# Coming blocks first on both sides of a weight change, and GpSimd makes the sums of coming weights, in a hybrid encoder step on one core

## The chip, the cores and the metric

The kernel runs on one core of a Trainium2 chip. The metric is the device time of one launch in microseconds. A core has a matrix engine (TensorE, in profiles PE; its weight loads are PEld), VectorE (DVE), ScalarE (ACT), GpSimd (POOL) and SyncE (SP, here a queue of DMA issues). Each engine runs its own list of instructions in order, and semaphores tie the lists together. SBUF is the on-chip memory, PSUM holds the eight banks into which TensorE adds its products.

## The reference

One layer of a streaming encoder for a prompt of 2048 tokens and a sample of 32 tokens, all in float32. The change touches only the combined input projection:

```
h = rmsnorm(x, p['norm1_w']) * (1 + sc1) + sh1
mq, mk, mv, mo, mi, mf, sq, sk, sv = split_proj(h @ p['w_in'])
...
q_b = rmsnorm(sq.reshape(B, T, SB_HEADS, SB_DIM), p['sb_q_norm_w'])
k_rows = rmsnorm(sk.reshape(B, T, SB_HEADS, SB_DIM), p['sb_k_norm_w'])
```

`h` has 1024 columns, `w_in` seven groups of 512 columns and eight gate columns. After it come the mLSTM heads, the stick-breaking attention, the output projection and the convolutional feed-forward part, which are the same before and after.

## The kernel before

Function `front` computes the projections. Group 0 of the weights is projected first, tile by tile (a tile is 128 tokens). The other six groups are taken in three pairs, (1,4), (5,3) and (6,2). Each pair is multiplied with the whole prompt in 8 units, so there are 24 units, w = 0 to 23. A unit takes two tiles of tokens and two groups of 512 columns as a 2 by 2 block product, and makes it of seven products instead of eight (Strassen's scheme in Winograd's form). The left factors are A11, A22, A12 and the sums S1 to S4 of quarters of `h`; the right ones, called cells here, are B11, B21, B22 and the sums T1 to T4 of quarters of the weights. The products are named P1 to P7 and stand on TensorE in the order P1, P5, P4, P6, P2, P7, P3.

Float32 is kept by parts: ScalarE copies a block to a rounded high part, VectorE subtracts it from the block for the low part, and a product is three passes (high by high, high by low, low by high) over four blocks of 128 rows, 12 matmuls. In each unit the left blocks of the next one are prepared: `left_sum_of` (VectorE), `left_high_of` (ScalarE), `left_low_of` (VectorE). The right blocks change only with the pair: `cell_high_of` and `cell_low_of` run in the unit before a change (w = 7 and 15, called leaving in the code: B11, T1, T4, T2) and in the first with new weights (w = 8 and 16, arriving: B21, T3, B22).

What ScalarE and VectorE do with the results: `seed_b` and `seed_c` copy a bank on which the next products build, `take_e`, `take_f` and `take_a` copy banks out, `add` makes the output tiles 1, 2 and 3 of a unit (tile 0 is the bank taken by `take_a`). From unit 8 on the tiles 0 and 2 are queries or keys of the attention. They are normalised by `norm_begin` (square and reduce) and `norm_end` (reciprocal and two products) on VectorE with `std` on ScalarE between. Then TensorE transposes them in the next unit (`turn`, four small matmuls, line 1354), ScalarE takes the high part (`take_turned`), VectorE the low part (`turned_low`, line 980), and GpSimd issues the two stores (`store_turned`). I write (w,0) and (w,1) for the two normalised tiles of unit w. A transpose waits for its tile, and also for the low part of the transpose before, since both use one bank:

```
pe.wait_ge(weighted, m + 1)
at_least(pe, turn_low, m)
```

The sums T1 to T4 of the next pairs' weights are made ahead, in eight events v = 0 to 7 in the units 0 to 5, 9 and 10. For each event SyncE loads four row blocks of weights (`load_event`, buffer `pw_rows`), TensorE multiplies the sample with them (`sample_product`, line 1366), VectorE overwrites them with the four sums (`event_sum`, line 899, 128x512 each), SyncE stores them (`store_event`, to `w_sums`), and the next load may be issued once the store has landed. Four more events, in units 11 to 14, have no sums. GpSimd fetches the sums and blocks back at a change (`renew`).

Nothing here is put in order by a scheduler: each engine's list is written out in the loops over w, and what stands in it is what the engine does next.

Of the kernel before, what the change touches and what calls it, by code (L numbers as in the profile page):

```python
# [124 lines left out]
def front(k, c, gc, dec, firstK, firstQ):  # L125
# [22 lines left out]
    LEFT_HIGHS = ("S1", "A11", "A22", "S2", "A12", "S3", "S4")  # L148
    LEFT_LOWS = ("A11", "A22", "S1", "A12", "S3", "S2", "S4")
# [78 lines left out]
    with ExitStack() as s:  # L228
# [77 lines left out]
        def product_of(w, name):  # L306

            return multiplied, 7 * w + PRODUCTS.index(name) + 1
# [62 lines left out]
        def _(sp):  # L371
# [57 lines left out]
            def store_out(w, j):  # L429
                if w >= FIRST and j in (0, 2):  # L430
                    sp.wait_ge(weighted, norm_tile(w, j // 2) + 1)
                elif j == 0:
                    sp.wait_ge(a_taken, w + 1)
                elif w < HALF and j in (1, 3):
                    sp.wait_ge(gated_out, 2 * w + j // 2 + 1)
                else:
                    sp.wait_ge(added, 3 * w + j)
# [69 lines left out]
            for w in range(UNITS):  # L507
# [18 lines left out]
                if w + 1 in EVENT_AT:  # L526
                    load_event(EVENT_AT[w + 1])
                store_out(w, 1)
# [3 lines left out]
                if w >= FIRST:  # L532
# [3 lines left out]
            store_out(UNITS - 1, 2)  # L536
# [9 lines left out]
        def _(act):  # L546
# [172 lines left out]
            for w in range(UNITS):  # L719
# [6 lines left out]
                if leaving:  # L726
                    cell_high_of(v, "B11")
                if arriving:
                    cell_high_of(w // HALF, "B21")
                if arriving and w > FIRST:  # L730
                    std(norm_tile(w - 1, 1))
                if more:
                    left_high_of("S1", n)
                take_e(w)
                if leaving:
                    cell_high_of(v, "T1")
                if arriving:
                    cell_high_of(w // HALF, "T3")
                if more:
                    left_high_of("A11", n)  # L740
                if w > FIRST:
                    take_turned(norm_tile(w - 1, 0))
                if more:
                    left_high_of("A22", n)
# [4 lines left out]
                if arriving:  # L749
                    cell_high_of(w // HALF, "B22")  # L750
                if more:
                    left_high_of("S2", n)
# [11 lines left out]
                if more:  # L764
                    left_high_of("A12", n)
                if w >= FIRST:
                    std(norm_tile(w, 0))
                if leaving:
                    cell_high_of(v, "T4")
                    cell_high_of(v, "T2")  # L770
                if more:
                    left_high_of("S3", n)
                if w < HALF:
                    gate_out(w, 1)
                if w >= FIRST and not leaving:
                    std(norm_tile(w, 1))
                if more:
                    left_high_of("S4", n)
# [8 lines left out]
        def _(dve):  # L787
# [100 lines left out]
            def event_sum(name, v_):  # L888
# [2997 lines left out]
```

## Time and profile before

| | us |
|---|---|
| median of 3 runs | 2980.31 (2975.06 to 2984.92) |
| the profiled execution | 2975.85 |
| its span | 2974.1 |
| TensorE busy | 2833.2, 95% of the span |
| VectorE busy | 2214.1, 74% |
| ScalarE busy | 1395.8, 47% |
| GpSimd busy | 556.2, 19% |

The time of an execution is the span plus what lies around it, here 1.75 us. The 24 units stand at 176.6 to 696 us of the span, and the attention begins at 709.4. A unit's first product P1 is the one written `pR<-pB,pA` after the product `pacc<-pB,pS` (P3) of the unit before. In the order of the units P5 is `pR<-pT,pS`, P4 `pR<-pT,pA`, P6 and P7 `pacc<-pT,pS`, and P2 again `pR<-pB,pA`. When products follow each other without a wait they start 2.72 us apart.

### The profile page before, as it was taken

To read this page: it belongs to the slowest core of one execution; us is meant where nothing else is said; L and a number is where in the kernel's file an instruction comes from. 1 tells how busy PE (TensorE), PEld (TensorE's weight loads), DVE (VectorE), ACT (ScalarE), POOL (GpSimd) and SP (SyncE) were. 2 spreads that over 40 slices of the span, in tenths; PEclk is the share of its full clock that TensorE was granted. 3 is DMA by queue.
4 is the path that set the end of the run, shared out by engine and by line. 5 is a ranking of instruction groups with operands and counts; after the bars stand their busy time and mean duration, and the time that the engine had idled before them with its cause. 6 is when DMAs were issued, how large, how long until landed. Compare 5 with 4: busy or idle time off the path is not lost.

```text
span 2974.1 us, 49846 instructions
## 1 busy us (share of the span) xinstructions
PE 2833.2 (95%) x16979; PEld 2446.7 (82%) x16979; DVE 2214.1 (74%) x3454; ACT 1395.8 (47%) x2729; POOL 556.2 (19%) x581
## 2 busy tenths in 40 slices
PE   6999999898999999999998999999999998999998
PEld 4777777686777888888887999999999997777776
DVE  3566687777998999796668777777877777887765
ACT  4644544435776888454555333333432224333332
POOL 3610011114666777220110000000000000000000
PEclk8999999998999999999999999999999999999999
DMA  7565666556422241696564444444667877655565
GB/s 267 200 222 201 211 234 203 184 177 159 128 59 59 60 99 43 216 338 195 187 215 161 150 150 150 152 153 153 209 219 230 262 235 254 195 189 188 179 209 186
DMA packets 359365, 541.47 MB, mean 182 GB/s; under 512 B 71058, under 2 KB 213976, under 8 KB 355478
## 3 DMA queue, kind: packets, MB, share of 16 engines
q1 hardware_dynamic: 337448, 467.81, 49.1%
q0 software_dynamic: 18112, 63.07, 6.2%
q10 hardware_dynamic: 3636, 8.45, 0.7%
q8 instruction: 93, 1.52, 0.2%
q14 instruction: 76, 0.62, 0.1%
HBM read 344.67 MB, written 194.55 MB: 181 GB/s over the span
## 4 chain that ended last, share of the span: by engine, by line
PE 45%; DVE 5%; DMA 5%; issue 1%; SPq 1%; ACT 1%; DVEq 0%; ACTq 0%
PE facc L3525 24%; PE facc L3655 6%; PE eacc L3504 6%; PE dacc L3655 4%; DMA y_out<-dres 1%; DMA fsums<-sums_d 1%; PE mpT L3678 1%; PE mpm L3687 1%; DVE fV L3036 1%; DMA w_out_plain<-w_out 1%; PE mpS L3697 1%; PE eyT L3487 1%; PE exT L3517 0%; DVE fV L3032 0%; DMA dsample_act<-act_d 0%
## 5 line engine op out<-in xcount | busy, mean ns | idle before, releaser
L3525 PE MATMUL facc<-fright,fsums 128*128 128x416 f32 x2112 | 419.3, 354 | 17.3 <-ACT facc L2591 7.2
L3525 PEld LDWEIGHTS facc<-fright,fsums 128*128 128x128 f32 x2112 | 398.7, 190 | 24.5 <-issue 16.3
L1720 DVE TENSOR_TENSOR_SCAN aC<-aB,aC,a 128x512 f32<-128x512 f32 (+3 forms) x326 | 362.8, 1113 | 12.5 <-ACT aB L1676 0.9
L1780 POOL TENSOR_TENSOR aS<-aS,aC 128x512 f32<-128x512 f32 (+3 forms) x326 | 335.0, 1035 | 154.0 <-DVE aC L1720 147.4
L3525 PE MATMUL facc<-fright,fwH 128*128 128x416 f32 x1056 | 290.1, 356 | 11.8 <-DVE fU L3020 9.9
L3525 PEld LDWEIGHTS facc<-fright,fwH 128*128 128x128 f32 x1056 | 199.3, 190 | 17.5 <-issue 12.2
L2980 DVE TENSOR_TENSOR fwL<-fraw,fwH 128x1024 fp32r<-128x1024 f32 x86 | 93.4, 1086 | 148.9 <-ACT fwH L2591 148.8
L2591 ACT ACTIVATE fU<-facc 128x416 f32<-128x416 f32 x132 | 67.4, 513 | 287.2 <-PE facc L3525 287.2
L1800 PE MATMUL a_z<-ak,aq 128*128 128x512 f32 (+2 forms) x616 | 199.7, 406 | 0.9 <-DMA ak<-qk_T 0.9
L1676 ACT ACTIVATE aB<-a_z 128x512 f32<-128x512 f32 (+3 forms) x326 | 180.3, 553 | 32.2 <-PE a_z L1800 18.9
L1826 PE MATMUL a_x<-ident,aS 128*128 128x128 f32 x1106 | 182.4, 281 | 10.5 <-ACT aA L1685 8.2
L3525 PE MATMUL facc<-fh,fwH 128*128 128x416 f32 x704 | 189.8, 351 | 0.0
L3525 PE MATMUL facc<-fright,fwL 128*128 128x416 f32 x528 | 186.4, 353 | 0.0
L1681 ACT ACTIVATE aS<-a_z 128x512 f32<-128x512 f32 (+3 forms) x326 | 182.2, 559 | 0.0
L1826 PEld LDWEIGHTS a_x<-ident,aS 128*128 128x128 f32 x1106 | 123.7, 141 | 53.9 <-issue 32.3
L1845 PEld LDWEIGHTS a_out<-aA,av 128*64 128x64 f32 x2176 | 123.4, 137 | 40.8 <-issue 31.0
L1845 PE MATMUL a_out<-aA,av 128*64 128x128 f32 x2176 | 155.2, 281 | 0.0
L1395 PE MATMUL pacc<-pT,pS 128*128 128x512 f32 x576 | 144.8, 401 | 5.6 <-DVE pT L911 2.9
L2591 ACT ACTIVATE dS<-dS_plain 128x512 fp32r<-128x512 f32 (+1 forms) x96 | 57.3, 597 | 187.1 <-DVE dS_plain L3109 61.9
L1395 PE MATMUL pR<-pB,pA 128*128 128x512 f32 x576 | 138.6, 389 | 1.3 <-issue 1.1
L547 ACT ACTIVATE pS<-pS_plain 128x512 fp32r<-128x512 f32 x96 | 60.7, 632 | 164.6 <-DVE pS_plain L928 63.2
L1395 PEld LDWEIGHTS pacc<-pT,pS 128*128 128x128 f32 x576 | 107.2, 191 | 35.5 <-issue 9.7
(438 smaller groups left out, 6351.3 us busy)
## 6 DMA issues: line engine op xcount, KB each, us to landing
sums_d<-fsums SPq DMA_DIRECT2D x88, 512.0 KB, 3.0
fsums<-sums_d SPq DMA_DIRECT2D x88, 512.0 KB, 4.6
fraw<-w_up SPq DMA_DIRECT2D x66, 512.0 KB, 4.1
proj_out<-pout SPq DMA_DIRECT2D x96, 256.0 KB, 4.3
ppart<-h_d SPq DMA_DIRECT2D x46, 512.0 KB, 4.6
dres<-x_d SPq DMA_DIRECT2D x92, 256.0 KB, 3.4
mwa<-w_ada SPq DMA_DIRECT2D x16, 1024.0 KB, 6.8
dpart<-act_d SPq DMA_DIRECT2D x32, 512.0 KB, 3.8
```

The source lines that it names most:

```text
L1395: op = mm_(banks[name], lefts[one][:, a, i], cell(other, b)[:, i], start=(name in ("P1", "P5", "P4") and i == 0 and m == 0), stop=(i == NK ...
L1676: nc.scalar.activation(part(B, RB, n), part(Z, NZ, n), ACT.Sigmoid, scale=-1.0).then_inc(pass_ready, 1)
L1681: nc.scalar.activation(part(S, RS, n), part(Z, NZ, n), ACT.Sigmoid).then_inc(stop_ready, 1)
L1720: v.tensor_tensor_scan(buf[:, a:b][:, ::-1], part(B, RB, n)[:, ::-1], nought[:, 0:width(n)], buf[:, b:b + 1], ALU.mult, ALU.add).then_inc( ...
L1780: nc.gpsimd.tensor_tensor(at, at, buf[:, a + 1:b + 1], ALU.mult).then_inc(w_ready, 1)
L1800: mm = nc.tensor.matmul(to, q[:, i * P:(i + 1) * P], keys[:, span], start=(half == 0), stop=(half == 1), skip_group_check=True)
L1826: mm = nc.tensor.transpose(X[:, n % NX, j * P:(j + 1) * P], src[:, j * P:(j + 1) * P], c["ident"][:])
L1845: mm = nc.tensor.matmul(O[e * SD:(e + 1) * SD, u % 2, at:at + P], V[:, h % 2, b], weight[:, j * P:(j + 1) * P], start=lead, stop=(g == 0 a ...
L2591: copy = lambda to, at: nc.scalar.activation(to, at, ACT.Copy)
L3504: mm = nc.tensor.matmul(acc[:, 1 - i.u, cols], a[:, i.u, kk], w[:, kk, cols], start=(kk == 0 and n == 0), stop=(kk == KD - 1 and n == len( ...
L3525: mm = nc.tensor.matmul(bank, a[:, kk], b[:, kk], start=(begins and kk == 0 and m == 0), stop=(kk == count - 1 and m == 2), skip_group_che ...
L3655: mm = nc.tensor.matmul(banks[name], a[:, i], b, start=(name in ("P1", "P5", "P4") and i == 0 and m == 0), stop=(i == len(WINDOW[w]) - 1 a ...
```

## The change

It has four parts.

1. In the two units of a weight change ScalarE and VectorE have another order. The coming cells and left blocks stand earlier (T1 on ScalarE after `take_f`, T3 right after B21, A12 and its like before T4, T2 after S3), and the high parts of units 8, 9, 16 and 17 are made in the order S1, A11, A22, A12, S2, S3, S4.
2. The tile (15,1) is normalised later in unit 16 and transposed after P1 of unit 17, not after P2 of unit 16. Its `take_turned` and `turned_low` stand at the head of unit 17. GpSimd fetches T4 for the last pair before it stores tile (14,0), and B21 before (14,1).
3. The last unit makes its products in the order P1, P4, P6, P2, P7, P5, P3, normalises tile 2 and adds it before the others, and stores as they come.
4. `event_sum` moves from VectorE to GpSimd. There the sums of events 0 to 3 stand after the stores of blank rows, those of 4 and 5 after `store_rows`, those of 6 and 7 after the stores of tiles (8,0) and (9,0).

```
+    CHANGE_HIGHS = ("S1", "A11", "A22", "A12", "S2", "S3", "S4")
+    LAST_PRODUCTS = ("P1", "P4", "P6", "P2", "P7", "P5", "P3")
...
@@ ScalarE, loop over the units @@
+                if w > FIRST and (w - 1) % HALF == 0 and w - 1 > FIRST:
+                    take_turned(norm_tile(w - 2, 1))
+                if leaving or arriving:
+                    if leaving:
+                        cell_high_of(v, "B11")
+                    else:
+                        cell_high_of(w // HALF, "B21")
+                        cell_high_of(w // HALF, "T3")
                     left_high_of("S1", n)
+                    take_e(w)
+                    if w > FIRST:
+                        take_turned(norm_tile(w - 1, 0))
+                    take_f(w)
+                    if leaving:
+                        cell_high_of(v, "T1")
+                    seed_c(w)
+                    if n in TAKEN_AT:
+                        take_sample(TAKEN_AT[n])
+                    if arriving:
+                        cell_high_of(w // HALF, "B22")
+                    left_high_of("A11", n)
+                    left_high_of("A22", n)
+                    if arriving and w > FIRST:
+                        std(norm_tile(w - 1, 1))
+                    take_a(w)
+                    if leaving and w > FIRST:
+                        take_turned(norm_tile(w - 1, 1))
+                    left_high_of("A12", n)
+                    left_high_of("S2", n)
+                    if leaving:
+                        cell_high_of(v, "T4")
+                    if w >= FIRST:
+                        std(norm_tile(w, 0))
+                    left_high_of("S3", n)
+                    if w < HALF:
+                        gate_out(w, 1)
+                    if leaving:
+                        cell_high_of(v, "T2")
+                    else:
+                        std(norm_tile(w, 1))
+                    left_high_of("S4", n)
+                    if w < HALF:
+                        gate_out(w, 3)
+                    continue
...
@@ VectorE, loop over the units @@
+                if w > FIRST and (w - 1) % HALF == 0 and w - 1 > FIRST:
+                    turned_low(norm_tile(w - 2, 1))
                 if leaving:
+                    left_sum_of(1, n)
+                    if w > FIRST:
+                        turned_low(norm_tile(w - 1, 0))
                     cell_low_of(n // HALF, "B11")
+                    cell_low_of(n // HALF, "T1")
+                    left_low_of("A11", n)
+                    left_low_of("A22", n)
+                    left_sum_of(2, n)
+                    left_low_of("S1", n)
+                    left_low_of("A12", n)
+                    if w >= FIRST:
+                        norm_begin(w, 0)
+                    if w > FIRST:
+                        turned_low(norm_tile(w - 1, 1))
+                    add(w, 1)
+                    add(w, 2)
+                    cell_low_of(n // HALF, "T4")
+                    left_sum_of(3, n)
+                    if w >= FIRST:
+                        norm_end(w, 0)
+                    cell_low_of(n // HALF, "T2")
+                    left_low_of("S3", n)
+                    add(w, 3)
+                    left_sum_of(4, n)
+                    left_low_of("S2", n)
+                    left_low_of("S4", n)
+                    continue
                 if arriving:
                     cell_low_of(w // HALF, "B21")
-                if arriving and w > FIRST:
-                    norm_begin(w - 1, 1)
-                if more:
                     left_sum_of(1, n)
...
                     cell_low_of(w // HALF, "T3")
+                    if w > FIRST:
+                        turned_low(norm_tile(w - 1, 0))
+                        norm_begin(w - 1, 1)
+                    cell_low_of(w // HALF, "B22")
                     left_low_of("A11", n)
+                    left_low_of("A22", n)
+                    left_sum_of(2, n)
+                    left_low_of("S1", n)
+                    left_low_of("A12", n)
+                    if w > FIRST:
+                        norm_end(w - 1, 1)
+                    norm_begin(w, 0)
+                    add(w, 1)
+                    add(w, 2)
+                    left_sum_of(3, n)
+                    left_low_of("S3", n)
+                    norm_end(w, 0)
+                    norm_begin(w, 1)
+                    add(w, 3)
+                    left_sum_of(4, n)
+                    left_low_of("S2", n)
+                    left_low_of("S4", n)
+                    continue
...
@@ GpSimd @@
+            for n in range(4):
+                event_sums(n)
             store_rows()
+            for n in range(4, NK + 2):
+                event_sums(n)
             for name in CELLS[len(AHEAD):]:
                 renew(1, name)
             for m in range(NORMS):
-                store_turned(m)
                 if m == norm_tile(2 * HALF - 2, 0):
                     renew(2, "T4")
+                store_turned(m)
+                if m in (0, 2):
+                    event_sums(NK + 2 + m // 2)
...
@@ TensorE, unit @@
-                for name in PRODUCTS:
+                for name in products(w):
...
+                    if name == "P1" and w % HALF == 1 and w - 1 > FIRST:
+                        turn(norm_tile(w - 2, 1))
-                    if name == "P5" and w > FIRST:
+                    if name == ("P5" if w < UNITS - 1 else "P4") and w > FIRST:
                         turn(norm_tile(w - 1, 0))
+                    if name == "P5" and w == UNITS - 1:
+                        turn(norm_tile(w, 0))
...
-                    if name == "P2" and w > FIRST:
+                    if name == "P2" and w > FIRST and w % HALF:
                         turn(norm_tile(w - 1, 1))
```

Three places in the lists show it. VectorE in unit 16, before, where the low part of the transposed tile (15,1) stands behind `norm_begin(16,0)`. The names are the left blocks (pA, pS), the squares (`pacc<-pout`), the low part (`pturn_low<-pacc`) and the output tiles (pout).

```order
L944 TENSOR_TENSOR pA<-ppart,pA 128x512
L961 TENSOR_TENSOR pacc<-pout 128x512
L963 TENSOR_REDUCE pnst<-pacc 128x8
L980 TENSOR_TENSOR pturn_low<-pacc,pturn 128x512
L954 TENSOR_TENSOR pout<-pE,pacc 128x512
L949 TENSOR_TENSOR pout<-pout,pacc 128x512
L933 TENSOR_TENSOR pS_plain<-ppart 128x512
L944 TENSOR_TENSOR pS<-pS_plain,pS 128x512
```

And now, at the end of unit 16 and the head of unit 17:

```order
L986 TENSOR_TENSOR pout<-pE,pacc 128x512
L967 TENSOR_TENSOR pS_plain<-ppart,pS_plain 128x512
L975 TENSOR_TENSOR pS<-pS_plain,pS 128x512 x2
L1001 RECIPROCAL pnst<-pnst 128x8
L1003 TENSOR_TENSOR pout<-pout,pnst 128x512
L1007 TENSOR_TENSOR pout<-pout,pnw 128x512
L1012 TENSOR_TENSOR pturn_low<-pacc,pturn 128x512
L959 TENSOR_TENSOR pS_plain<-ppart 128x512
L975 TENSOR_TENSOR pA<-ppart,pA 128x512
```

The low part has moved behind the whole of unit 16 and behind `norm_end(16,1)`, and stands right ahead of the first left sum of unit 17.

TensorE from the last product of unit 16 into unit 17, before:

```order
L1395 MATMUL pacc<-pB,pS 128x512 x12
L1395 MATMUL pR<-pB,pA 128x512 x12
L1395 MATMUL pR<-pT,pS 128x512 x12
L1354 MATMUL pacc<-ident,pout 128x128 x4
L1395 MATMUL pR<-pT,pA 128x512 x12
```

And now:

```order
L1483 MATMUL pacc<-pB,pS 128x512 x12
L1483 MATMUL pR<-pB,pA 128x512 x12
L1442 MATMUL pacc<-ident,pout 128x128 x4
L1483 MATMUL pR<-pT,pS 128x512 x12
L1442 MATMUL pacc<-ident,pout 128x128 x4
L1483 MATMUL pR<-pT,pA 128x512 x12
```

A second transpose stands in unit 17 ahead of P5, that of (15,1); the one after P5, of (16,0), waits for its low part.

GpSimd from the stores of blank rows on, before:

```order
L1188 DMA proj_out<-pblank 96x512 x6
L1193 DMA ug_d<-pturn 68x128 x4
L1195 DMA m_out<-pm_end 8x1x1
L1212 DMA pT_plain<-w_sums 128x4x512 x2
L1212 DMA pB_plain<-w_in 128x4x512
```

And now (`pw_rows` are the rows of weights that become their sums):

```order
L1268 DMA proj_out<-pblank 96x512 x6
L1245 TENSOR_TENSOR pw_rows<-pw_rows 128x512 x16
L1273 DMA ug_d<-pturn 68x128 x4
L1275 DMA m_out<-pm_end 8x1x1
L1245 TENSOR_TENSOR pw_rows<-pw_rows 128x512 x8
L1292 DMA pT_plain<-w_sums 128x4x512 x2
L1292 DMA pB_plain<-w_in 128x4x512
L1292 DMA pT_plain<-w_sums 128x4x512
L1292 DMA pB_plain<-w_in 128x4x512
L1283 DMA qk_T<-pturn 128x4x128
L1284 DMA qk_T<-pturn 128x4x128
L1245 TENSOR_TENSOR pw_rows<-pw_rows 128x512 x4
```

Sixteen sums come in, then eight, then twice four behind the two DMAs of a transposed tile.

## Rows read from the trace of the kernel before

**Rows 1.** Busy time by stretches: stretch, length, busy us (instructions), granted clock, DMA.

```profile
core 0: us, PE busy (x) PEld busy (x) DVE busy (x) ACT busy (x) POOL busy (x), PEclk, DMA share, GB/s
340.50:366.20 25.70, 20.15 (x85) 15.46 (x84) 20.37 (x21) 16.39 (x20) 0.75 (x1) 1.00 0.47 159
...
494.30:521.50 27.20, 22.75 (x93) 18.45 (x92) 20.09 (x29) 11.82 (x19) 5.66 (x8) 0.87 0.54 176
521.50:552.60 31.10, 23.01 (x93) 18.13 (x92) 25.28 (x29) 17.53 (x22) 3.08 (x5) 0.89 0.61 219
552.60:573.20 20.60, 20.47 (x94) 16.51 (x93) 14.24 (x25) 10.64 (x18) 2.99 (x4) 1.00 0.50 160
...
595.30:675.90 80.60, 80.58 (x369) 66.18 (x368) 62.69 (x105) 32.39 (x64) 11.95 (x16) 1.00 0.55 170
```

**Rows 2.** TensorE's timeline in unit 8: start, duration, instruction, [idle before, releaser].

```profile
359.35 3.00 PE L1395 MATMUL pacc<-pT,pS 128*128 128x512 f32 x12 [2.94 <-DVE pT L911]
```

**Rows 3.** TensorE's timeline in units 15 and 16.

```profile
513.00 1.09 PE L1354 MATMUL pacc<-ident,pout 128*128 128x128 f32 x4 [4.45 <-DVE pturn L980]
513.74 5.18 PE L1395 MATMUL pacc<-pT,pS 128*128 128x512 f32 x12
...
533.96 1.11 PE L1354 MATMUL pacc<-ident,pout 128*128 128x128 f32 x4 [6.84 <-DVE pout L975]
534.73 4.95 PE L1395 MATMUL pR<-pT,pA 128*128 128x512 f32 x12
```

**Rows 4.** Timelines of VectorE, SyncE's queue and TensorE, units 0 and 1.

```profile
193.85 2.74 DVE L899 TENSOR_TENSOR pw_rows<-pw_rows 128x512 f32<-128x512 f32 x4
...
196.62 0.33 SPq L427 DMA_DIRECT2D w_sums<-pw_rows  x1
...
200.56 1.76 SPq L421 DMA_DIRECT2D pw_rows<-w_in  x4
...
207.48 1.07 PE L1366 MATMUL pR<-pw_rows,h_plain 128*32 128x256 f32 x16
```

**Rows 5.** GpSimd's timeline, the first projection and unit 9.

```profile
105.86 1.29 POOL L1167 TENSOR_TENSOR pT_plain<-pturn,pT_plain 128x512 f32<-128x512 f32 x1
107.22 1.30 POOL L1169 TENSOR_TENSOR pT_plain<-pturn,pT_plain 128x512 f32<-128x512 f32 x1
...
380.85 0.75 POOL L1204 DMA_DIRECT2D qk_T<-pturn  x1
```

**Rows 6.** Timelines of GpSimd and VectorE, first projection.

```profile
143.50 4.68 POOL L1157 TENSOR_TENSOR h1L<-h_plain,h1H 128x1024 fp32r<-128x1024 f32 x1
149.75 2.37 POOL L1157 TENSOR_TENSOR h1L<-h_plain,h1H 128x1024 fp32r<-128x1024 f32 x1 [1.57 <-DMA h_d<-h_plain]
...
143.63 2.34 DVE L885 TENSOR_TENSOR pT<-pT_plain,pT 128x1024 fp32r<-128x1024 f32 x2
```

**Rows 7.** Timelines of SyncE's queue and TensorE, units 9 and 10.

```profile
367.99 1.85 SPq L421 DMA_DIRECT2D pw_rows<-w_in  x4
...
374.94 1.07 PE L1366 MATMUL pR<-pw_rows,h_plain 128*32 128x256 f32 x16
...
389.19 1.96 SPq L421 DMA_DIRECT2D pw_rows<-w_in  x4
...
396.53 1.07 PE L1366 MATMUL pR<-pw_rows,h_plain 128*32 128x256 f32 x16 [0.24 <-DMA pw_rows<-w_in]
```

**Rows 8.** VectorE's timeline, units 15 to 17.

```profile
502.51 0.69 DVE L975 TENSOR_TENSOR pout<-pout,pnw 128x512 f32<-128x512 f32 x1
...
547.41 2.28 DVE L911 TENSOR_TENSOR pB<-pB_plain,pB 128x2048 fp32r<-128x2048 f32 x1
549.61 0.68 DVE L944 TENSOR_TENSOR pS<-pS_plain,pS 128x512 fp32r<-128x512 f32 x1
550.21 0.68 DVE L944 TENSOR_TENSOR pA<-ppart,pA 128x512 fp32r<-128x512 f32 x1
...
562.49 0.69 DVE L975 TENSOR_TENSOR pout<-pout,pnw 128x512 f32<-128x512 f32 x1
```

**Rows 9.** Timelines of ScalarE and VectorE, last unit.

```profile
683.88 0.58 ACT L547 ACTIVATE pacc<-pR 128x512 f32<-128x512 f32 x1
...
701.87 0.69 DVE L980 TENSOR_TENSOR pturn_low<-pacc,pturn 128x512 fp32r<-128x512 f32 x1 [1.90 <-ACT pturn L547]
```

More of the change, by code:

```diff
@@ L436, in store_out @@
                 else:
-                    sp.wait_ge(added, 3 * w + j)
+                    sp.wait_ge(added, 3 * w + (2 if j == 1 and w == UNITS - 1 else j))
                 sp.dma_start(d["proj_out"][group_of(w, j), tok(tile_of(w, j)), :], out(w, j)).then_inc(out_stored[j][w % 2], 16)
@@ L741, in _ @@
+                if not more:
+                    take_turned(norm_tile(w - 1, 0))
+                    take_f(w)
+                    seed_c(w)
+                    take_a(w)
+                    take_turned(norm_tile(w - 1, 1))
+                    std(norm_tile(w, 0))
+                    std(norm_tile(w, 1))
+                    take_e(w)
+                    break
+                left_high_of("S1", n)
+                take_e(w)
+                left_high_of("A11", n)
                 if w > FIRST:
@@ L742, in _ @@
                     take_turned(norm_tile(w - 1, 0))
-                if more:
-                    left_high_of("A22", n)
+                left_high_of("A22", n)
                 take_f(w)
@@ L748, in _ @@
                     take_sample(TAKEN_AT[n])
[L749 to L752, printed above, removed]
+                left_high_of("S2", n)
                 if w == 4:
@@ new lines, in _ @@
+                    norm_end(w, 0)
[5 more added lines that the diff above has]
+                    continue
+                if not more:
+                    turned_low(norm_tile(w - 1, 0))
+                    norm_begin(w, 0)
+                    norm_end(w, 0)
+                    turned_low(norm_tile(w - 1, 1))
+                    add(w, 2)
+                    norm_begin(w, 1)
+                    norm_end(w, 1)
+                    add(w, 1)
+                    turned_low(norm_tile(w, 0))
+                    add(w, 3)
+                    turned_low(norm_tile(w, 1))
+                    break
@@ L1078, in _ @@
+                left_sum_of(1, n)
+                left_low_of("A11", n)
                 if w > FIRST:
                     turned_low(norm_tile(w - 1, 0))
-                if arriving and w > FIRST:
-                    norm_end(w - 1, 1)
-                if more:
-                    left_low_of("A22", n)
+                left_low_of("A22", n)
                 if TAKEN_AT.get(w, NN) < NN:
                     sample_squares(TAKEN_AT[w])
-                if more:
-                    left_sum_of(2, n)
@@ L1137, in _ @@
                     gate_columns()
-            norm_end(UNITS - 1, 1)
-            for m in range(NORMS - 2, NORMS):
-                turned_low(m)
         @block.gpsimd
@@ L1425, in _ @@
                 unit(w)
-            for m in range(NORMS - 2, NORMS):
-                turn(m)
+            turn(NORMS - 1)
     k.keep(first_head_in)
```

118 lines of the change are left out of this document (44 added, 74 removed).

## The prediction, as it was made before the result was known

> **What bounds the kernel now.** All the edits lie in the first projections, 176.6 to 709.4 us, so I read the busy time by stretches first. The reader should see TensorE within half a microsecond of full in the long steady stretches, and idle time in four places: 25.70 us for 20.15 us of work around unit 8, 27.20 for 22.75 in unit 15, 31.10 for 23.01 in unit 16 [rows 1], and a tail after the last unit. A steady unit without weight rows takes 20.1 us (80.60 us for four, same rows); in the two bad units the granted clock falls to 0.87 and 0.89. So TensorE bounds the stage, and only what ends a TensorE wait counts. Next, TensorE in order of time. At the first change of weights the longest wait is 2.94 us, for VectorE's low half of T3 [rows 2]. At the second, a transpose waits 4.45 us for another transpose's low half and one waits 6.84 us for a normalised tile; the product after the first took 5.18 us where 3.0 is usual [rows 3]. The losses are 6.7 us (25.7 less 19.0) in unit 8, 7.0 in unit 15 and 10.9 in unit 16. Last I read what feeds these, VectorE and the queues.
>
> **The change, part by part.** Times below are absolute positions in the trace of before, and D is how much later TensorE stands.
>
> *The sums of coming weights.* VectorE made four in 2.74 us beginning right at the end of the row product [rows 4]. GpSimd needs 1.30 each for the same size, 5.2 us [rows 5]. In units 1 to 5 VectorE reached its sums some microseconds late, so GpSimd, which starts when the product ends, is as early. Not in unit 0: there VectorE began at 193.85, so GpSimd ends near 199.2 instead of 196.59. The chain behind it has no slack: sums, store issued at 196.62, next load at 200.56 (3.9 later), product at 207.48 [rows 4]. In SyncE's queue nothing else holds that load by then. D after unit 1 is +2.6. From below: the rows may have landed up to 0.6 before they were used, and GpSimd may be as quick as VectorE, which gives 0; from above 3.2, if the first of the four takes half a microsecond more.
>
> In units 9 and 10 GpSimd must first store a transposed tile, because its list has store_turned(0) and (2) ahead of the sums. It issued the second of its two DMAs at 380.85 [rows 5], so the four sums run from 381.6 to 386.8 at best. VectorE works beside them. The row of a GpSimd difference that took 4.68 us, against 2.37 alone, while VectorE made two differences of 1.17, shows the two in turn and not at once [rows 6]. VectorE has one or two such instructions to make here (an A12 low half, the squares), so I take +1.6: 388.4. The store lands 3.9 later, 392.3, against a load issued at 389.19. TensorE used these rows at 396.53 after a wait for them [rows 7]: D +3.0 here. The ends are 1.4, without the collision, and 3.8, with twice of it. The same chain in unit 10 comes out only 0.2 to 1 us later than before, which a TensorE already 3 us late does not feel. What VectorE saves (2.74 us eight times) buys nothing, since TensorE did not wait for VectorE in those units.
>
> The Trainium skill (SBUF — State Buffer, section Who interferes with whom) says that a VectorE instruction with two SBUF inputs and a GpSimd instruction that reads SBUF exclude each other for the whole instruction. The trace agrees, 4.68 being 2.37 plus 2.34 us; without contention this term would be 1.6 us smaller, +1.4 in place of +3.0.
>
> *First change, units 7 to 9.* ScalarE now takes T4 some 1.6 us earlier, but T2 only after S3 and a gate, and S4, the second gate and seed_b(8) stand behind T2. P6 and P2 of unit 8 so start about 1.4 us later than before. T3's high half then follows B21's at once on ScalarE, and its low half stands ahead of A11 on VectorE; P7 starts at 357.6 instead of 359.35 [rows 2], P3 and unit 9 also 1.8 us earlier. Then its first transpose waits 1 us for a tile that VectorE normalises at the old time. Then the rows of weights: those of unit 9 were requested at 367.99 and used at 374.94 [rows 7], and that request stands behind the third left sum, which moves by +0.3. I take 0, with ends -1.8 and +0.6.
>
> *Second change, units 15 to 17.* First what goes: the left sum and the turned low half come ahead of B11 and T1 on VectorE, so the 4.45 us wait goes and with it the slow P7 (5.18 for 3.0). TensorE ends unit 15 at 514.2 instead of 521.5. From here VectorE sets the pace. Its instructions step at 0.60 (512 wide) and 2.20 (2048 wide: 547.41 to the next at 549.61), a norm_begin takes 1.34, a norm_end 1.57 [rows 8]. Its list from the end of norm_end(14,1), 502.51 + 0.6 = 503.1: sum 0.6; a wait until 505.5, while ScalarE does S1 (0.78 after the sum's start), E and the turned tile at 0.5 each; turned low 0.6; B11, T1 4.5; five short and a pause 3.2; norm_begin 1.3; turned low and two adds 1.8; T4 2.2 (519.1); sum, norm_end 2.2 (521.3); T2 when ScalarE has done S3 and T2, 522.3, to 524.5; S3, add, sum 2.0; then S4 and seed_b on ScalarE end at 527.5. P6 of unit 16 starts at 527.65, 3.0 late. ScalarE's B21 takes 1.84, and the low half 2.2: 531.6, P2. sum, T3 low: 534.4. ScalarE reaches B22 behind T3, S1, E, the turned tile, F, the seed and the sample at 535.2, and ends at 537.1; B22's low half ends at 539.35, against 547.41 + 2.28 = 549.69 before [rows 8]. TensorE is 10.3 us ahead there, with waits of 1.7, 3.0, 1.2, 0.5 and 1.7 us behind it.
>
> Now what is late next. In unit 17 the second transpose, of tile (16,0), may write its bank only when the low half of (15,1) has been taken. That low half now stands behind VectorE's whole rest of unit 16. Before, from A12's low half at 550.21 to the last instruction of norm_end(16,1), 562.49, plus 0.61, are 12.9 us [rows 8]. The new list adds norm_end(15,1), 1.57; the low half only changes its place; and A11, A22, a sum and S1 ahead of A12 add 2.6. That is 17.05: 539.35 becomes 556.4. TensorE gets to that transpose at 539.45 + 8.65 (P3, P1, a transpose, P5; 2.72 a product) = 548.1, and stands 8.4 us. And what follows runs at half clock, as after the 6.84 us wait: a transpose of 1.1 us and a P4 of 4.95 [rows 3]. The transpose starts at 556.5, P4 at 557.3, P6 at 562.1, P2 at 564.8, a transpose, P7 and P3 end at 573.4, where unit 18 starts; before it started at 573.2 [rows 1]. So all of the 10.3 us is given back. Term +0.2. The ends: -4 if the clock holds and VectorE's list is 1.5 us shorter, +3 if the waits of unit 16 also slow a product or the fetch of T4 or B22 is late. Nothing hides this wait: behind the transpose TensorE has P4, and P4 needs only what is long ready.
>
> *The last unit.* P6 comes third instead of fourth. It needs seed_b, which ended on ScalarE at 684.46 [rows 9], and so starts at 684.60 as before, while P5, which used to fill 678.6 to 681.3, now comes after P7. TensorE ends 2.7 us later. Against it, tile 2 is added and normalised without waiting for P3; the last transpose waits for the low half of (23,0), 700.4, and the last low half starts at 702.2 against 701.87 [rows 9]. +0.4, with ends -2 and +2.7.
>
> **Sum.** 2.6 + 3.0 + 0 + 0.2 + 0.4 = +6.2 us. The profiled execution took 2975.85 us, 1.75 of it outside the span; the sum on it is 2982.1. The median of before is 2980.31, 4.5 above that execution, so a median of the new kernel should be 2986.5, +0.2%. About 0.3% (9 us) is what a measurement can tell here from no change.
>
> **Rivals.**
> *The second change keeps its gain.* The low half of (15,1) would be taken in time, or TensorE would meet it within a couple of microseconds. Then the 10.3 us stay, the 2 us that unit 18 takes over a steady unit (22.1 against 20.1) go, and if GpSimd's sums land in time too the 5.6 us as well: 2975.85 + 6.2 - 12.3 - 5.6, about 2964 on the profiled execution, 2968 as a median. For it: the two long waits of rows 3 do disappear. Against it: the count of VectorE's list above, which needs no guess at a new duration. 0.2.
>
> *The clock falls in units 16 and 17 (slower).* Five waits of 0.5 to 3 us stand within 20 us, then 8.4 us. In the trace the granted clock was 0.89 of 31 us where the single wait was 6.84 [rows 1, 3], and full around unit 8 with 2.94. If four more products go at 5.2 instead of 3.0 us that is +9, and +3 from late rows and the end: 2975.85 + 6.2 + 12, as a median 2998. It decides once two of the products P6, P2, P7 and P3 of unit 16 take over 4 us. 0.2.
>
> *The moved sums cost nothing.* The rows land as before, because GpSimd starts the moment the product ends and the copies have slack that I don't see. Then +0.6: 2981. For it: units 1 to 5. Against it: the three visible waits for these rows of 0.2 to 0.7 us. 0.15.
>
> My forecast has 0.45. Split by the 9 us bound, with the run-to-run spread of the three runs (10 us): the first rival is faster in nearly all of its 0.2, the second slower in all of its 0.2, and the forecast's own range, 2978 to 2994, puts 0.04 beyond the slower side. Faster 0.19, within 0.3% 0.56, slower 0.25. The range that leaves out one tenth on either side reaches to the rivals' values, 2968 to 2998.
>
> **What would show it.** TensorE's row product of unit 1 at about 210 and waiting for its rows; that of unit 10 near 402; the product after unit 15's transpose at full clock; a transpose in unit 17 that waits some 8 us for a turned low half on VectorE, its product P4 slow; P6 of the last unit waiting 2.9 us for ScalarE. I am wrong if unit 17's transpose waits under 3 us, or if rows of weights cause no wait.

## The result and the profile after

| | before | changed |
|---|---|---|
| median of 12 runs each, us | 2980.07 | 2983.90 |
| the profiled execution, its span, us | 2975.85, 2974.1 | 2986.12, 2984.4 |
| ratio of the times, 95% interval | | 1.002 (1.001 to 1.0029) |

The changed kernel is 0.2% slower, within the 0.3% that I called no change. One of its twelve executions took 4592 us at a granted clock of 0.56; it is left out of the ratio, and without it the median is 2983.50. Of the 10.3 us between the two profiled spans 7.6 lie in the stretch that the change touches (from TensorE's first P1 of unit 0 to the attention's first matmul, 532.86 us before and 540.48 after). 2.6 lie ahead of any edit: unit 0 starts at 179.19 instead of 176.59, and over the executions of this study that start moved between 175.6 and 181.1. I therefore compare lengths from here on, not positions.

The page's first part, of the changed kernel. GpSimd has gained 46.6 us of busy time, and VectorE has lost only 3.5 of its 2214.1, though it gave up eight times 2.74 us [rows 4]:

```profile
## 1 busy us (share of the span) xinstructions
PE 2833.7 (95%) x16979; PEld 2446.8 (82%) x16979; DVE 2210.6 (74%) x3422; ACT 1396.8 (47%) x2729; POOL 602.8 (20%) x613
```

Busy time by stretches of the changed kernel, cut at its own units: 0 and 1, 8, 9 to 11, then 15, 16, 17, 18, and 23 up to the attention. Columns as in [rows 1]:

```profile
179.19:226.86 47.67, 42.97 (x201) 33.01 (x201) 26.89 (x42) 20.71 (x35) 16.07 (x17) 0.96 0.64 225
...
347.19:371.70 24.51, 19.95 (x86) 15.46 (x84) 17.22 (x17) 15.21 (x19) 0.75 (x1) 1.00 0.48 172
371.70:442.47 70.77, 64.58 (x325) 50.42 (x324) 61.27 (x88) 26.19 (x52) 19.63 (x19) 1.00 0.61 203
506.27:526.27 20.00, 20.00 (x93) 16.55 (x92) 17.12 (x25) 12.63 (x19) 4.24 (x6) 1.00 0.83 267
526.27:554.44 28.17, 22.27 (x89) 16.77 (x88) 24.54 (x28) 15.74 (x21) 4.51 (x6) 0.94 0.61 212
554.44:584.77 30.33, 22.17 (x97) 18.11 (x96) 20.40 (x35) 12.32 (x21) 3.55 (x5) 0.89 0.36 117
584.77:604.77 20.00, 20.00 (x93) 16.55 (x92) 15.61 (x27) 8.09 (x16) 2.89 (x5) 1.00 0.49 159
...
684.77:719.67 34.90, 23.12 (x102) 18.38 (x100) 19.16 (x33) 6.93 (x15) 7.51 (x12) 0.89 0.42 136
```

The same lengths, unit by unit (distance from P1 to the next unit's P1), of both kernels and of the experiments, tell where each microsecond is. Units 12 to 14 take 63.8 to 64.1 in all.

| length, us | 0, 1 | 2 to 7 | 8 | 9 to 11 | 15 | 16 | 17 | 18 | 19 to 22 | 23 and tail | all |
|---|---|---|---|---|---|---|---|---|---|---|---|
| before | 42.94 | 120.98 | 25.69 | 64.29 | 27.23 | 31.09 | 20.56 | 22.08 | 80.66 | 33.54 | 532.86 |
| changed | 47.67 | 120.33 | 24.51 | 70.77 | 20.00 | 28.17 | 30.33 | 20.00 | 80.00 | 34.90 | 540.48 |
| changed again | 46.71 | 119.88 | 24.51 | 70.68 | 20.00 | 28.17 | 30.66 | 20.00 | 80.00 | 33.33 | 538.05 |
| e1 | 42.94 | 120.63 | 24.48 | 66.07 | 20.00 | 28.15 | 31.24 | 20.00 | 80.00 | 33.73 | 531.04 |
| e2 | 46.79 | 120.86 | 25.99 | 68.42 | 27.40 | 31.08 | 20.54 | 22.13 | 80.37 | 33.13 | 540.51 |
| e3 | 45.86 | 120.02 | 24.49 | 70.83 | 20.00 | 28.20 | 23.54 | 22.10 | 80.38 | 34.78 | 534.00 |
| e4 | 48.81 | 120.07 | 24.50 | 70.90 | 20.00 | 28.15 | 30.95 | 20.00 | 80.00 | 32.72 | 539.90 |
| e5 | 43.86 | 120.89 | 24.48 | 66.18 | 20.00 | 28.21 | 23.52 | 22.10 | 80.37 | 33.37 | 526.78 |
| e6 | 42.90 | 120.64 | 22.28 | 65.88 | 20.00 | 26.45 | 24.25 | 21.40 | 80.38 | 33.59 | 521.85 |
| e7 | 42.95 | 119.98 | 24.52 | 66.03 | 20.00 | 28.14 | 30.20 | 20.00 | 80.00 | 34.97 | 530.59 |

Read changed against before: +4.7 in units 0 and 1, -1.2 in unit 8, +6.5 in 9 to 11, then -7.2 and -2.9 in 15 and 16, +9.8 in 17, -2.1 and -0.7 behind it, +1.4 at the end.

TensorE's waits in the whole stage of the changed kernel, first part of that view (what was waited for: us in total, times, longest):

```profile
PE pacc L1483 <- ACT pacc L559: 9.3, 4, 3.0
PE pacc L1442 <- DVE pturn_low L1012: 8.2, 1, 8.2
PE pR L1454 <- DMA pw_rows<-w_in: 7.0, 5, 3.1
PE pacc L1442 <- DVE pout L1007: 4.2, 4, 1.5
```

The rows of weights were waited for 1.2 us in all before and now 7.0; one transpose waits 8.2. The places of both in TensorE's timeline:

```profile
213.23 1.69 PE L1454 MATMUL pR<-pw_rows,h_plain 128*32 128x256 f32 x16 [3.09 <-DMA pw_rows<-w_in]
...
382.67 1.07 PE L1454 MATMUL pR<-pw_rows,h_plain 128*32 128x256 f32 x16 [1.11 <-DMA pw_rows<-w_in]
...
406.51 1.07 PE L1454 MATMUL pR<-pw_rows,h_plain 128*32 128x256 f32 x16 [1.29 <-DMA pw_rows<-w_in]
...
429.94 1.07 PE L1454 MATMUL pR<-pw_rows,h_plain 128*32 128x256 f32 x16 [1.10 <-DMA pw_rows<-w_in]
...
533.41 0.66 PE L1442 MATMUL pacc<-ident,pout 128*128 128x128 f32 x4 [1.54 <-DVE pout L1007]
...
539.80 4.24 PE L1483 MATMUL pacc<-pT,pS 128*128 128x512 f32 x12 [2.98 <-ACT pacc L559]
543.91 3.31 PE L1483 MATMUL pR<-pB,pA 128*128 128x512 f32 x12
...
551.60 3.00 PE L1483 MATMUL pacc<-pB,pS 128*128 128x512 f32 x12 [1.38 <-issue]
...
568.70 1.09 PE L1442 MATMUL pacc<-ident,pout 128*128 128x128 f32 x4 [8.16 <-DVE pturn_low L1012]
569.44 4.14 PE L1483 MATMUL pR<-pT,pA 128*128 128x512 f32 x12
...
693.31 4.18 PE L1483 MATMUL pacc<-pT,pS 128*128 128x512 f32 x12 [2.50 <-ACT pacc L559]
```

The first four are the row products of units 1, 9, 10 and 11. The waits of [rows 3] are gone, and in unit 16 (526.27 to 554.44) stand 1.54, 2.98 and 1.38 us instead. The transpose at 568.70 is that of (16,0); the 8.16 us ahead of it are the largest wait of the stage. P6 at 693.31 is that of the last unit, waiting for ScalarE's seed.

### The profile page after: what moved, and what is told of

The parts are those of the page before. It is cut to its first block, busy times and chain, and to the rows that moved or that the text cites. A ratio compares the mean times of both kernels' runs of the same rounds, so it can differ in the third digit from the quotient of the medians.

```text
span 2984.4 us, 49870 instructions
## 1 busy us (share of the span) xinstructions
PE 2833.7 (95%) x16979; PEld 2446.8 (82%) x16979; DVE 2210.6 (74%) x3422; ACT 1396.8 (47%) x2729; POOL 602.8 (20%) x613
## 4 chain that ended last, share of the span: by engine, by line
PE 46%; DVE 5%; DMA 5%; issue 1%; SPq 1%; ACT 1%; DVEq 0%; ACTq 0%
PE facc L3616 24%; PE facc L3746 6%; PE eacc L3595 6%; PE dacc L3746 4%; DMA y_out<-dres 1%; DMA fsums<-sums_d 1%; PE mpT L3769 1%; DMA dres<-x_d 1%; DVE fV L3127 1%; DMA w_out_plain<-w_out 1%; PE mpm L3778 1%; PE mpS L3788 1%; PE eyT L3578 1%; DVE fV L3123 0%; DVE fV L3132 0%
## 5 line engine op out<-in xcount | busy, mean ns | idle before, releaser
L1917 PE MATMUL a_x<-ident,aS 128*128 128x128 f32 x1106 | 182.1, 281 | 10.1 <-ACT aA L1776 8.2
```

What stands on the lines that cost most here:

```text
L1917: mm = nc.tensor.transpose(X[:, n % NX, j * P:(j + 1) * P], src[:, j * P:(j + 1) * P], c["ident"][:])
```

## The experiments

The changed kernel was built up and taken apart in pieces. The lengths are in the table above. Ratios are to the kernel before.

**The changed kernel once more**, for the spread of its lengths.

> The changed kernel as it is, run beside the next three on one chip, since e3 and e4 came out 4 to 6 us faster in time than the length of their units says. If that is a matter of the chip, this run is near +0.1% here with a stage of 540.5 us; if it belongs to e3 and e4, it is at +0.2% again.

2981.37 us, ratio 1.001 (1.000 to 1.002), stage 538.05. Of the stage's lengths units 8 and 15 to 22 repeat within 0.4 us, units 0 and 1 and the tail differ by 1.0 and 1.6. The two stages differ by 2.4 us, so a single execution tells the stage no better than that, and single units between 15 and 22 much better. The run was also to show whether the times of e3 and e4, below, are better than their stages for a reason of the chip. It came out at the +0.1% named for that case, but its interval also holds the +0.2% of the other, so it does not decide.

**e1: the sums back on VectorE**, all else as changed.

```
@@ VectorE, in the other units @@
+    event = EVENT_AT.get(w, SUMMED)
+    if event < SUMMED:
+        for name in ("T1", "T3", "T2", "T4"):
+            event_sum(name, event)
@@ GpSimd @@
-    for n in range(4):
-        event_sums(n)
     store_rows()
-    for n in range(4, NK + 2):
-        event_sums(n)
...
-    if m in (0, 2):
-        event_sums(NK + 2 + m // 2)
```

> The changed kernel with the event sums back on VectorE, in its place of before (behind S1's low half); all else as changed. Theory (the moved sums cost about 9 us: 4.4 in unit 1, 4 to 5 around units 9 to 11): no wait for rows over 0.8 us, no VectorE instruction of 3.6 us, the 24 units and what follows to the attention take 540.5 - 9 = 531.5 us, and the time is about 1.5 us under before. Rival (the new order at the changes costs it, the sums nothing): the stage stays near 540 and the time near +0.2%.

2973.21 us, ratio 0.9978 (0.9966 to 0.9989), stage 531.04. Against the changed kernel units 0 and 1 give back 4.7 us and units 9 to 11 another 4.7: the whole loss by GpSimd's sums, 9.4 us, where the prediction had 5.6. The stage fits the expected 531.5, the time is further under before than expected (6.6 us for 1.5). Of the waits for rows 0.96 us in unit 9 stays, more than the 0.8 that I had allowed, so that one comes with the new order of the first change. The 8.21 us wait in unit 17 stays, and so do the gains of 15 and 16.

**e2: the kernel before, with the sums on GpSimd**, the same edit in the other direction.

```
@@ VectorE @@
-    if event < SUMMED:
-        for name in ("T1", "T3", "T2", "T4"):
-            event_sum(name, event)
@@ GpSimd @@
+    for n in range(4):
+        event_sums(n)
     store_rows()
+    for n in range(4, NK + 2):
+        event_sums(n)
...
+    if m in (0, 2):
+        event_sums(NK + 2 + m // 2)
```

> The kernel before with one edit: the event sums on GpSimd, placed as in the changed kernel. Theory: unit 1 waits some 3 us for its rows, units 10 and 11 about 1 to 2 us each for rows and for the normalised tile; the stage takes 532.9 + 9 = 542 us, the time is +0.3% on before. Rival (the sums are hidden without the new order): stage 533 to 535, time as before.

2985.32 us, ratio 1.0023 (1.0012 to 1.0033), stage 540.51, 7.7 above before: +3.9 in units 0 and 1, +4.1 in 9 to 11, together 8.0. TensorE's row product of unit 1 in this kernel:

```profile
214.48 1.94 PE L1373 MATMUL pR<-pw_rows,h_plain 128*32 128x256 f32 x16 [2.47 <-DMA pw_rows<-w_in]
216.35 3.54 PE L1402 MATMUL pacc<-pT,pS 128*128 128x512 f32 x12
```

It waits for the rows, and is itself slow (1.94 for 1.07 us), as is the product behind it. So the late rows of units 1, 10 and 11 come with the fourth part of the change alone (units 10 and 11 wait 1.18 and 1.09 us for them here).

**e3: the low part of (15,1) earlier**, behind the third left sum of unit 16, with ScalarE's copy of it. Nothing else differs from the changed kernel.

```
@@ ScalarE, unit 17 and unit 16 @@
-    if w > FIRST and (w - 1) % HALF == 0 and w - 1 > FIRST:
-        take_turned(norm_tile(w - 2, 1))
...
     take_a(w)
+    if arriving and w > FIRST:
+        take_turned(norm_tile(w - 1, 1))
@@ VectorE, unit 17 and unit 16 @@
-    if w > FIRST and (w - 1) % HALF == 0 and w - 1 > FIRST:
-        turned_low(norm_tile(w - 2, 1))
...
     left_sum_of(3, n)
+    if w > FIRST:
+        turned_low(norm_tile(w - 1, 1))
```

> The changed kernel, but the low half of the transposed tile (15,1) (with ScalarE's copy) stands inside unit 16's list, behind the third left sum, not at the head of unit 17. Theory: the 8.2 us wait of the transpose (16,0) falls to about 2.3, until norm_end(16,0) is done; its P4 runs at full clock; stage 540.5 - 6.8 = 533.7, the time equals before to 0.05%. Rival (VectorE is simply behind here, whatever the order): the wait stays above 6 us or comes back as a wait of P6, stage 539 or more.

2975.73 us, ratio 0.9989 (0.9979 to 0.9999), stage 534.00. TensorE's timeline in unit 17:

```profile
559.17 0.66 PE L1442 MATMUL pacc<-ident,pout 128*128 128x128 f32 x4 [1.94 <-DVE pout L1007]
559.58 3.01 PE L1483 MATMUL pR<-pT,pA 128*128 128x512 f32 x12
...
581.27 0.66 PE L1442 MATMUL pacc<-ident,pout 128*128 128x128 f32 x4 [1.01 <-DVE pout L1007]
```

Busy time of units 16 and 17 of e3, columns as above, at full clock in both:

```profile
523.00:551.13 28.13, 20.75 (x89) 15.69 (x88) 24.50 (x28) 15.70 (x21) 4.52 (x6) 1.00 0.62 217
551.13:574.67 23.54, 21.18 (x98) 16.77 (x97) 17.67 (x31) 11.42 (x20) 2.99 (x4) 1.00 0.45 151
```

One subtraction of 0.69 us moved up on VectorE, and ScalarE's copy with it, takes the wait from 8.16 to 1.94 us and P4 from 4.14 to 3.01. Unit 17 is 6.8 us shorter. Unit 18 is 2.1 longer again, with the wait of 1.01 us that stood there before and that the changed kernel did not have: while TensorE stands for 8 us VectorE catches up with it, and where it does not stand, VectorE is late again one unit on. I had not allowed for that: with 2.5 us back in units 18 to 22 the early low part is worth 4.3 us and not 6.8, and the stage fits the expected 533.7 because units 0 and 1 happened to take 1.8 us less here, which the edit does not touch.

**e4: the last unit in its old order**, the rest as changed.

```
-    return PRODUCTS if w < UNITS - 1 else LAST_PRODUCTS
+    return PRODUCTS
@@ VectorE, last unit @@
-    norm_end(w, 0)
...
+    norm_end(w, 0)
+    add(w, 1)
...
+    add(w, 3)
```

> The changed kernel with the last unit's products in the order of before (P1, P5, P4, P6, P2, P7, P3), its lists following. Theory: the 2.5 us wait of P6 and the slow product behind it go, a wait of 3.5 us for the last transposes comes back; stage 540.5 - 1.4 = 539.1, not to be told from the changed kernel by time. Rival (the new last order gains in the tail what it loses at P6): stage 541 or more.

2981.95 us, ratio 1.0005 (0.9994 to 1.0016), stage 539.90. From the last P1 to the attention it takes 32.72 us. Over all the runs of the table that length is 33.54, 33.13, 32.72, 33.37 and 33.59 with the old order (mean 33.3) and 34.90, 33.33, 33.73, 34.78 and 34.97 with the new one (mean 34.3). So the new order costs about 1.1 us in the mean, less than its own spread. The waits alone do not say why, since they come to nearly the same: the old order waits 3.44 to 3.47 us for the last transpose, the new one 1.02 or 1.03 there and 2.50 to 2.69 for the seed ahead of P6. What differs is the speed of P6 behind that wait. It took 2.98 and 2.96 us in the changed kernel once more and in e1, with 33.33 and 33.73 us to the attention, as in the old order. It took 4.18, 4.29 and 4.49 in the changed kernel, e3 and e7, with 34.90, 34.78 and 34.97. The stage of e4 is only 0.6 us under the changed kernel's, between the expected 539.1 and the rival's 541, because units 0 and 1 took 48.81 us in this execution.

**e5: e1, e3 and e4 in one kernel**: of the change there remains the new order of both weight changes, with the low part early.

> The changed kernel with three parts taken back or put right: sums on VectorE, the low half of (15,1) in unit 16, the last unit in its old order. Theory (the three terms add): stage 531.0 - 6.5 - 0.6 = 524 us, 9 us under before, time -0.3% or better. Rival (VectorE has the sums to make again and catches TensorE at another place): stage 528 or more.

2969.73 us, ratio 0.9972 (0.9959 to 0.9985), stage 526.78 for an expected 524, between that and the rival's 528. 0.9 of the difference is a wait for rows in unit 0, which no other run with VectorE's sums had; another 1.8 was in the expectation, which took e3's gain with its short units 0 and 1. The pieces add up: from the changed kernel's 540.5, 8.4 go in the sums' units, 6.8 in unit 17, 1.5 at the end, 2.5 come back in units 18 to 22, and 0.6 in 2 to 7.

**e6: e5 with B21 ahead of S4.** The wait of 2.98 us ahead of P6 in unit 16, and of 2.30 in unit 8, is for `seed_b`, which stood behind S4 on ScalarE. Here it and B21's high part come ahead of S4.

```
@@ ScalarE @@
-    seed_b(w)
+    if not arriving:
+        seed_b(w)
...
-    cell_high_of(w // HALF, "B21")
...
+    seed_b(n)
+    cell_high_of(v, "B21")
     left_high_of("S4", n)
```

> e5 with ScalarE's seed_b and the high half of B21 for the first unit with new weights ahead of S4 in the unit before. Theory: at the second change B21's low half no longer waits for ScalarE (1.6 us idle of VectorE in the changed kernel) and P6 waits 0.5 us less; stage 1.5 to 2 us under e5, 522. Rival (the fetched B21 lands late, or VectorE's count alone sets the pace): stage as e5 or longer.

2966.27 us, ratio 0.9962 (0.9948 to 0.9976), stage 521.85. This kernel is faster than both: by 0.4% than before, and by 0.5% than the changed one as measured on the same chip (0.9962 to 1.001). TensorE around P6 of units 8 and 16:

```profile
353.84 3.02 PE L1494 MATMUL pacc<-pT,pS 128*128 128x512 f32 x12 [1.28 <-DVE pS L988]
...
529.51 3.02 PE L1494 MATMUL pacc<-pT,pS 128*128 128x512 f32 x12 [2.46 <-DVE pS L988]
532.41 2.98 PE L1494 MATMUL pR<-pB,pA 128*128 128x512 f32 x12
...
550.98 0.66 PE L1453 MATMUL pacc<-ident,pout 128*128 128x128 f32 x4 [1.98 <-DVE pout L1020]
551.39 4.58 PE L1494 MATMUL pR<-pT,pA 128*128 128x512 f32 x12
```

The waits ahead of P6 now name VectorE's low part of a left sum, since S4's high part comes later, and they are shorter by 1.0 and 0.5 us. The other 1.2 us in each come behind P6: P2 starts 2.90 us after it, where in the changed kernel it starts 4.11 after (543.91 less 539.80), held by B21, whose low part ends on VectorE at 543.80. 0.7 of it went again in unit 17, where the product after the transpose took 4.58 us.

**e7: only the sums of events 1 to 5 on GpSimd**, those of 0, 6 and 7 on VectorE.

```
@@ VectorE @@
-    if event < SUMMED:
+    if event < SUMMED and event not in [1, 2, 3, 4, 5]:
@@ GpSimd @@
+    event_sums(1)
+    event_sums(2)
+    event_sums(3)
     store_rows()
+    event_sums(4)
+    event_sums(5)
```

> e1 with the sums of events 1 to 5 on GpSimd, those of 0, 6 and 7 on VectorE. Theory: these five are hidden on either engine, stage as e1, 531.0 within 0.5, no wait for rows in units 2 to 4. Rival (each moved sum costs TensorE something): 3 to 5 us more than e1.

2973.48 us, ratio 0.9986 (0.9976 to 0.9997), stage 530.59, as e1, and no wait for rows stands in units 2 to 4. These five are hidden on either engine; the loss is made by the three events (0, 6 and 7) whose chain has no slack.

## Why the prediction was right, and where it was not

The time came out as forecast (2983.9 for 2986.5, by the sum +6.2 us in the stage for a measured +7.6 and, once more, +5.2). That the number is so near is in part luck. The sums on GpSimd cost 8.0 to 9.4 us where I had 5.6, and the last unit 1.0 more than forecast in this execution; a gain of 2.7 us behind unit 17, which the forecast did not have, made up for about half of that.

*Sums in units 0 and 1, +2.6.* The chain went as described and GpSimd began on time, 17.26 us after unit 0's P1 as VectorE had. But it took longer:

```profile
196.45 6.07 POOL L1245 TENSOR_TENSOR pw_rows<-pw_rows 128x512 f32<-128x512 f32 x4 [2.88 <-PE pR L1454]
...
389.12 5.95 POOL L1245 TENSOR_TENSOR pw_rows<-pw_rows 128x512 f32<-128x512 f32 x4
```

6.07 us, not the 5.2 of four times 1.30 [rows 5]. SyncE's queue stored them at once and requested the next rows 4.2 us later:

```profile
202.54 0.33 SPq L437 DMA_DIRECT2D w_sums<-pw_rows  x1
...
206.69 1.76 SPq L431 DMA_DIRECT2D pw_rows<-w_in  x4
```

The row product came 3.15 us later than before, at the upper end that I gave (3.2). On top the clock fell: granted 0.96 over units 0 and 1, and the product that waited took 1.69 us for 1.07, the P6 behind it 4.01. Together +4.7. The five executions with all sums on GpSimd have +2.9 (e3), +3.8 (changed again), +3.9 (e2), +4.7 and +5.9 (e4), and the two lowest are those in which no product behind the wait was slow. The term was mis-sized by 0.3 to 3.3 us, and a fall of the clock stood only in the rival about units 16 and 17.

*Units 9 and 10, +3.0, and unit 11, nothing.* This is the step that failed. e1 isolates it: without GpSimd's sums units 9 to 11 take 66.07 us, with them 70.77, +4.7. Unit 9 hardly differs (23.36 and 23.52). Unit 10 has +2.5 for my +3.0, and unit 11 has +2.0 for nothing. I had written that the chain in unit 10 comes "only 0.2 to 1 us later than before, which a TensorE already 3 us late does not feel". It came later still, and unit 11 waits 1.10 us for its rows and 0.84 for a tile. GpSimd's sums in unit 10 took 5.94 us, as in unit 9, and VectorE lost time as well, where I had let it save 2.74 us an event. VectorE of the changed kernel in unit 9, beside the sums of 389.12 to 395.07:

```profile
388.62 3.60 DVE L975 TENSOR_TENSOR pS<-pS_plain,pS 128x512 fp32r<-128x512 f32 x1
392.14 1.77 DVE L975 TENSOR_TENSOR pA<-ppart,pA 128x512 fp32r<-128x512 f32 x1
393.83 1.78 DVE L993 TENSOR_TENSOR pacc<-pout 128x512 f32<-128x512 f32 x1
395.65 0.69 DVE L995 TENSOR_REDUCE pnst<-pacc 128x8 f32<-128x512 f32 x1
```

The same instructions in e1, with VectorE's own sums among them:

```profile
382.82 0.69 DVE L988 TENSOR_TENSOR pS<-pS_plain,pS 128x512 fp32r<-128x512 f32 x1
383.43 2.74 DVE L943 TENSOR_TENSOR pw_rows<-pw_rows 128x512 f32<-128x512 f32 x4
386.09 0.68 DVE L988 TENSOR_TENSOR pA<-ppart,pA 128x512 fp32r<-128x512 f32 x1
386.69 0.69 DVE L1006 TENSOR_TENSOR pacc<-pout 128x512 f32<-128x512 f32 x1
387.42 0.69 DVE L1008 TENSOR_REDUCE pnst<-pacc 128x8 f32<-128x512 f32 x1
```

From the start of the first to the start of the reduction it is 7.03 us with the sums on GpSimd and 4.60 with them on VectorE. VectorE is slower for having given the work away. The three instructions lost 5.1 us together and the sums would have cost 2.7. That comes back as the transposes' waits in units 10 and 11 (0.98 and 0.84 us, both for a normalised tile of VectorE; e2 has 0.94 and 0.93, e1 and e7 none there), and with the rows' waits of 1.29 and 1.10 it makes 4.2 of the +4.5.

The Trainium skill (SBUF — State Buffer, section Who interferes with whom) says that a VectorE instruction with two inputs in SBUF contends with a GpSimd instruction that reads SBUF, and that one with at most one SBUF input, outside the 2-port modes, does not. The rows agree in unit 9: the three with two SBUF inputs took 3.60, 1.77 and 1.78 us. The reduction started after GpSimd's end and tells nothing. VectorE beside the group of unit 0 (196.45 to 202.52) has both kinds:

```profile
197.51 0.78 DVE L975 TENSOR_TENSOR pA<-ppart,pA 128x512 fp32r<-128x512 f32 x1 [0.97 <-ACT pA L559]
199.29 0.69 DVE L986 TENSOR_TENSOR pout<-pE,pacc 128x512 f32<-128x512 f32 x1 [1.00 <-PE pacc L1483]
199.90 0.68 DVE L981 TENSOR_TENSOR pout<-pout,pacc 128x512 f32<-128x512 f32 x1
```

The two adds with an input in PSUM (`pacc`) took their usual time, as the skill has it. But the difference with two SBUF inputs took only 0.78 us here for 1.77 in unit 9, so what such an instruction loses is not fixed, and no run shows what sets it. I had used that rule for GpSimd's end and not for VectorE's.

*First change, 0.* Right within its ends. P6 of unit 8 starts 1.8 us later than before (forecast 1.4) and P7 1.3 earlier (1.8), so unit 8 is 1.2 us shorter; in e1, which has no delay by the sums, unit 9 takes 2.1 back, with waits of 0.89 us for a tile and 0.96 for rows. Units 8 to 11 of e1 are 0.6 us longer than before's, the upper end that I gave. No run undid this part alone, so that split rests on e1's and before's lengths.

*Second change, +0.2.* Right in size and in place. Unit 15 at 20.0 us (-7.2, forecast -7.3), P6 of unit 16 waits 2.98 (3.0), units 15 and 16 together -10.1 (-10.3), the transpose in unit 17 waits 8.16 (8.4) and P4 takes 4.14 (4.95), so units 15 to 17 together are -0.4. The count of VectorE's list held. The transpose of (16,0) started 42.43 us after unit 16's P1, and by the prediction's positions 42.3 (556.5 less 514.2). Why that is so late shows on VectorE in the changed kernel:

```profile
549.21 2.29 DVE L942 TENSOR_TENSOR pB<-pB_plain,pB 128x2048 fp32r<-128x2048 f32 x1 [0.67 <-ACT pB L559]
551.42 1.29 DVE L975 TENSOR_TENSOR pA<-ppart,pA 128x512 fp32r<-128x512 f32 x2
...
567.26 0.69 DVE L1007 TENSOR_TENSOR pout<-pout,pnw 128x512 f32<-128x512 f32 x1
567.87 0.68 DVE L1012 TENSOR_TENSOR pturn_low<-pacc,pturn 128x512 fp32r<-128x512 f32 x1
```

From the end of B22's low half at 551.4 VectorE works without an idle time of a microsecond until the low part, which starts at 567.87 and is done 17.1 us after that end; I had 17.05. e3, which moves nothing but this low part and its copy, shows that it is their place in the lists.

*Units 18 to 22, nothing.* -2.7 measured. The wait of 8 us lets VectorE catch up, so the small waits of units 18 and 19 go; e3 and e5, without the long wait, have them again. The prediction put this gain with the rival in which unit 17 does not wait, which is the wrong way round.

*The last unit, +0.4.* The named wait came, 2.50 us for 2.9, and the length is between the ends that I gave: +1.4 in this execution, about +1.1 as a mean over ten. In the two executions with P6 at its usual speed it is -0.2 and +0.2 of before's; the rest is the slow P6, which the term did not have.

*The rivals.* The second change did not keep its gain. The clock fell in one product of unit 16 (P6, 4.24 us), not in two, so that rival stayed short of its own condition. That one product cost nothing either: unit 16 took 28.17 us with it and 28.20 in e3, where its granted clock was full, since P2 waits for B21 in any case. Even in e4, with P6 at 5.46 us, the unit took 28.15. The moved sums cost 8.0 (e2 against before) to 9.4 us (against e1), not nothing.

What stays open: e1, e3 and e4 are by their times 4 to 6 us better than their stages say (e1: -6.6 us by the ratio, -1.8 by the stage), while e2 and e6 agree within 1 us, and in e5, e7 and the changed kernel once more the time is about 2 us better than the stage. The rest of the program, from the attention on, is the same code, but took 2258 to 2265 us in the single profiled executions of the study. So one execution cannot place those 5 us, and their cause stays open.

## What to carry to other kernels

Before work is moved from one elementwise engine to the other, look at what the giver does meanwhile and at how many inputs its instructions read from SBUF: in unit 9 VectorE gave 2.7 us of work away and lost 5.1 beside it. Ask of each moved block not its busy time but the chain behind it: all eight have a store and a load behind them, and for five of them that chain has slack, so that they could go to either engine at no cost that shows; for three it has none, and these cost 8 to 9 us. And when a wait on a shared buffer is moved into a later unit, count the list of the engine that frees it down to the instruction that frees it; one subtraction made 8.5 us earlier was worth 6.8 us in its unit, and 4.3 when the next five units are counted.

## What the runs showed of the hardware that I had not expected

A VectorE difference of 128x512 took 3.60 us instead of 0.69 when it met GpSimd's sums, 2.8 times the 1.30 us of one GpSimd operation, though it had started 0.5 us before them. GpSimd's four took 5.6 to 6.4 us over the eight events, for 5.2.

The half clock (1.2 GHz) does not follow from the length of a single wait. P6 of unit 16 took 4.24 us after 2.98 in the changed kernel, and P7 of unit 8 took 3.0 after 2.94 before [rows 2]. P6 of the last unit took 4.18 after 2.50 in the changed kernel; here it is in e1:

```profile
683.72 2.96 PE L1494 MATMUL pacc<-pT,pS 128*128 128x512 f32 x12 [2.54 <-ACT pacc L559]
```

The wait is the same and the clock full. P4 of unit 17 was at full clock after 1.94 us in e3 and took 4.58 after 1.98 in e6. The widest spread is P6 of unit 16 behind waits of 2.96 to 2.98 us: 2.98 in the changed kernel once more and in e3, 4.24 to 4.58 in the changed kernel, e5, e1 and e7, and 5.46 in e4. So the same wait made the product behind it 1.2 to 2.5 us longer in one execution than in another, and a wait of 2 to 3 us should be priced with up to 2.5 us behind it, unless something else is waited for there anyway.
